# Gates of the dense tokens: from one-hot matrix products to an accumulating scatter by GpSimd

## The chip, the cores and the metric

One core of a Trainium2 chip runs the whole kernel. The metric is the device time of one execution in microseconds. Before the change it is 4364.05 us, the median of 3 runs (4363.18 to 4364.18).

## What is computed

One inference step of one layer for 576 tokens: 512 prompt tokens and 64 sample tokens, width 2048. Attention and a pooling branch come first; the change lies in the expert mixer behind them:

```python
s = einsum('nhcd,hckd->nhck', q, sub_keys)          # 8 heads, 2 halves, 128 keys
sv, si = top_k(s, 16)
cand = sv[:, :, 0, :, None] + sv[:, :, 1, None, :]  # 256 sums a head
top_s, top_p = top_k(cand, 16)
experts = take_along_axis(cidx, top_p)              # a * 128 + b, of 16384 experts
gate = softmax(top_s)
act = gelu(einsum('nd,nhkd->nhk', h, u[experts]))
out = einsum('nhk,nhkd->nd', gate * act, v[experts])
```

So each token has 8 x 16 = 128 chosen experts with a gate each. Two heads may choose the same expert; then their gates add up.

## The kernel before

The expert part treats the tokens in three ways. For the first 384 (**dense tokens**, TV) it computes the activation of all 16384 experts, multiplies it by a gate that is zero where an expert was not chosen, and multiplies that by all values. For tokens 384 to 447 it computes all activations too but picks single cells of them later. For the last 128 (N_SU) it gathers the 128 chosen rows of u and of v one row per token at a time.

**Expert stage.** 128 expert tiles (N_U), one for each second key b, each of 128 experts. For a tile SP loads 1 MB of u (line 577), VectorE turns it (`turn`, line 1643), ScalarE rounds it to the high part (line 1138), VectorE subtracts for the low part (`u_low`, line 1648), and TensorE runs 48 matmuls (`expert_tile`, line 2309) of 448 columns. ScalarE applies gelu and SP stores the result to gelu_dram (line 582). Everything is double buffered: u_high of tile n+1 waits for the matmuls of tile n-1. The parts stand in each engine's program in an order written out by hand.

In tiles 0 to 34, seven for each of the five blocks of 128 tokens, VectorE also does the selection (lines 1655 to 1716) in the order `SEL_ORDER = (3, 4, 0, 1, 2)`, a piece behind each half tile. The result for a block is `sel`: first key a, second key b and gate, token by chosen slot. TensorE turns each block (`turn_selected`, line 2325) and ScalarE copies it to iaT, ibT and gT.

From tile 36 on two things run beside the tiles:

- **Dots**: GpSimd gathers a row of u for each of 128 tokens (`gather_u`, line 791, a ring of 3 buffers; each gather waits for the dot that frees its buffer) and VectorE multiplies and sums it (`dot`, line 1778). `dots_of` spreads the 128 dots over 88 tiles (D_TILES).
- **Gate groups**: `groups_of` spreads 96 groups of 4 dense tokens over 83 tiles. VectorE writes, for each token, a one-hot matrix of a and a matrix of b weighted with the gate (lines 1766 and 1770). TensorE multiplies the two in the middle of an expert tile (`gate_matrix`, line 2344), which gives the token's 128x128 gates with equal experts summed. ScalarE copies the group out (`take_gates`, line 1170), and SP stores 48 pieces of 512 KB to gmat_dram (line 596).

**Value stage.** For each expert tile SP loads the gelu values and the gates of the dense tokens (lines 620 to 622), VectorE multiplies them (line 1810), and TensorE runs three matmuls of 384 columns for each of 16 output blocks (line 2387). GpSimd's gathers of rows and cells (lines 806 to 820) run beside it.

Ahead of the expert stage stand the branch products (16 weight tiles, G_BR), the output product (16, G_OUT) and the query product (16, G_PQ), whose weights SP loads in one sequence (`load_tile`).

Of the kernel before, what the change touches and what calls it, by code (L numbers as in the profile page):

```python
# [18 lines left out]
F = mybir.dt.float32  # L19
# [36 lines left out]
NTOK_G = 4  # L56
# [4 lines left out]
N_G = TV // NTOK_G  # L61
GB = 64
# [22 lines left out]
N_HALF = TV * 2 // GB  # L85
G_PER_HALF = GB // 2 // NTOK_G
G_TILES, D_TILES = 83, 88
# [7 lines left out]
def groups_of(n):  # L95
    n -= DOT_TILE
    return range(N_G * n // G_TILES, N_G * (n + 1) // G_TILES) if 0 <= n < G_TILES else ()


PIECES = {1 + [n for n in range(N_U) if g in groups_of(n)][0] + 1 + i: (m, i)  # L100
          for m in range(N_HALF) for g in [G_PER_HALF * (m + 1) - 1] for i in range(4)}


NQ, QR = 4, 32
H_EARLY = PK * GB // T
# [14 lines left out]
def hybrid_step(nc, x_prompt, x_sample, cache_k, cache_v, state_pool, page_table, norm1_g, w_in, b_gate,  # L120
# [4 lines left out]
    with ctx:  # L125
# [143 lines left out]
        ssum = r("ssum", [P, 2, PH])  # L269
        r = Region(x2, END)  # L270
        one_i = [r(f"one_i{s}", [P, NTOK_G, PK]) for s in range(2)]
        gate_j = [r(f"gate_j{s}", [P, NTOK_G, PK]) for s in range(2)]
        u_rows = [r(f"u_rows{i}", [P, D]) for i in range(U_RING)]
        assert r.at - BASE <= END - 4096
        gmat = [Region(A_MAIN + s * PK * GB * 2, A_RING)(f"gmat{s}", [P, PK, GB // 2]) for s in range(2)]
        turned = [Region(A_MAIN + PK * GB * 4, A_RING)("turned0", [P, KD // 2, P]), Region(END - 4096, END)("turned1", [P, KD // 2, P])]

# [9 lines left out]
        g_back = [None, r("g_back1", [P, N_HALF, 2, GB // 2])]  # L287
# [8 lines left out]
        g_back[0] = r("g_back0", [P, N_HALF, 2, GB // 2])  # L296
# [37 lines left out]
        gmat_dram = nc.dram_tensor("gmat_dram", [P, N_PAIR, N_HALF, 2, GB // 2], F).ap()  # L334
# [3 lines left out]
        u_tiles = peer_u.rearrange("l (e c j) d -> (l c) e j d", c=QR, j=PK)  # L338
        gelu_cells = gelu_dram.rearrange("j i t -> (j i t)").unsqueeze(1)
# [50 lines left out]
        oh_v, gm_mm, gm_ev = (sem(n) for n in ("oh_v", "gm_mm", "gm_ev"))  # L390
        gm_out = [sem(f"gm_out{s}") for s in range(2)]
# [140 lines left out]
        def _(sp):  # L532
# [58 lines left out]
            def store_gates(n):  # L591
                if n in PIECES:
                    m, piece = PIECES[n]
                    j, at = slice(piece * PK // 4, (piece + 1) * PK // 4), slice(piece * PK // 8, (piece + 1) * PK // 8)
                    sp.wait_ge(gm_ev, G_PER_HALF * (m + 1))
                    sp.dma_start(gmat_dram[:, at, m].rearrange("i j x t -> i j (x t)"),
                                 gmat[m % 2][:, j, :].rearrange("i (j x) t -> i j (x t)", x=2)).then_inc(gm_out[m % 2], 16)

            for n in range(N_U - 4):
                if n:  # L600
                    store_gelu(n - 1)
                sp.wait_ge(u_turn, 2 * (n + 3))
                load_u(n + 4, n % 2)
                store_gates(n)
            for n in range(N_U - 4, N_U - 2):
                store_gelu(n - 1)
                store_gates(n)
# [7 lines left out]
            def load_weights(k):  # L615
# [5 lines left out]
                sp.dma_start(g_back[k % 2][:, :, :, :], gmat_dram[:, k]).then_inc(ag_in[0], 16)  # L621
                sp.dma_start(a_back[1][:, :], gelu_dram[2 * k + 1][:, 0:TV]).then_inc(ag_in[1], 16)

            for s in range(2):
                sp.wait_ge(gm_out[s], 64 * (TV // GB))
# [49 lines left out]
        def _(pool):  # L675
# [91 lines left out]

            for s in range(2):
# [97 lines left out]
        def _(act):  # L866
# [284 lines left out]
            def take_selected(tb):  # L1151

                w = tokens(tb)
                act.wait_ge(sel_tmm, SEL_AT[tb] + 1)
# [9 lines left out]
            def take_gates(g):  # L1164

# [1310 lines left out]
```

## Time and profile before

| | us |
|---|---|
| runs, median of 3 | 4364.05 |
| span of the profiled execution | 4361.2 |
| TensorE busy | 4257.0 (98%) |
| VectorE busy | 2941.9 (67%) |
| ScalarE busy | 1218.7 (28%) |
| GpSimd busy | 742.2 (17%) |
| expert stage | about 1870 to 3190 |
| value stage | about 3190 to 4330 |

The span runs from the first to the last instruction of the profiled execution; that execution has no other time of its own, and its span is 2.9 us under the median of the runs. PE is TensorE's matmuls, PEld its weight loads, DVE VectorE, ACT ScalarE, POOL GpSimd, SP SyncE. The chain that ended last is followed back from the last instruction to whatever released it. Spans on GpSimd are rough. A number in brackets behind an instruction is the idle time before it and what ended that.

### The profile page before, as it was taken

The numbers are of one execution on the slowest core, as the hardware profiler recorded it, in microseconds if no ns is written. First come the engines' busy times: TensorE is split into PE (matmuls) and PEld (weight loads), VectorE is DVE, ScalarE is ACT, GpSimd is POOL, SyncE is SP. The second block draws the span as 40 slices with busy tenths as digits, with TensorE's granted clock in tenths as the row PEclk, the third lists the DMA queues.
The fourth block names the chain that finished last, engine by engine and source line by source line (L and its number), as shares of the span: only waits on it lengthen the run. The fifth ranks groups of instructions, "written<-read, shape, count | busy, mean of one in ns | idle before, by whom it ended". The sixth has DMA issues, their size and how long they took to land.

```text
span 4361.2 us, 67488 instructions
## 1 busy us (share of the span) xinstructions
PE 4257.0 (98%) x28439; PEld 4024.2 (92%) x28439; DVE 2941.9 (67%) x4423; ACT 1218.7 (28%) x1610; POOL 742.2 (17%) x745
## 2 busy tenths in 40 slices
PE   7999999999999989999999999999999999999998
PEld 7999888998899989989999999999989999999998
DVE  3232463322334356699989999999868888888887
ACT  3221353322212121123232222222222222222234
POOL 1001002332000000000011111111122443333320
PEclk9999999999999989999999999999999999999999
DMA  6433226676343544345589999999999999999993
GB/s 195 113 102 106 85 63 196 227 244 204 110 133 116 149 104 85 78 118 131 129 243 292 292 282 297 280 292 289 278 329 356 359 338 361 364 355 356 356 344 131
DMA packets 599373, 968.32 MB, mean 222 GB/s; under 512 B 143889, under 2 KB 406033, under 8 KB 565016
## 3 DMA queue, kind: packets, MB, share of 16 engines
q1 hardware_dynamic: 508560, 519.33, 41.9%
q0 software_dynamic: 84992, 434.18, 27.0%
q10 hardware_dynamic: 5520, 10.49, 0.8%
q8 instruction: 225, 3.69, 0.3%
q14 instruction: 76, 0.62, 0.0%
HBM read 873.63 MB, written 85.75 MB: 220 GB/s over the span
## 4 chain that ended last, share of the span: by engine, by line
PE 94%; DVE 3%; ACT 1%; issue 1%; DMA 1%; SPq 0%; ACTq 0%; DVEq 0%
PE pair L1968 29%; PE pair L2309 28%; PE pair L2387 24%; PE quad L1968 2%; PE pair L2344 2%; PE pair L1932 1%; PE quad L2369 1%; PE quad L1932 1%; PE quad L2139 1%; ACT w_hi L890 1%; PE pair L2004 1%; PE quad L2182 1%; PE quad L2279 0%; PE quad L2054 0%; SPq L534 0%
## 5 line engine op out<-in xcount | busy, mean ns | idle before, releaser
L2309 PE MATMUL pair<-act_hi,w_hi 128*128 128x448 f32 x2048 | 757.0, 370 | 4.4 <-DVE w_lo L1648 4.4
L2309 PE MATMUL pair<-act_lo,w_hi 128*128 128x448 f32 x2048 | 748.9, 366 | 0.0
L2309 PE MATMUL pair<-act_hi,w_lo 128*128 128x448 f32 x2048 | 748.6, 366 | 0.0
L1968 PE MATMUL pair<-act_hi,w_hi 128*128 128x288 f32 x3264 | 719.0, 302 | 29.2 <-DVE act_lo L1353 12.2
L1293 DVE TENSOR_TENSOR w_lo<-w_raw,w_hi 128x2048 fp32r<-128x2048 f32 x103 | 236.2, 2293 | 746.7 <-ACT w_hi L890 746.7
L1968 PE MATMUL pair<-act_hi,w_lo 128*128 128x288 f32 x3264 | 702.6, 297 | 0.0
L1968 PE MATMUL pair<-act_lo,w_hi 128*128 128x288 f32 x3264 | 701.3, 297 | 0.0
L2387 PE MATMUL pair<-wx_hi,v_hi 128*128 128x384 f32 x2016 | 678.8, 337 | 5.5 <-DVE wx_lo L1817 3.3
L2387 PE MATMUL pair<-wx_hi,v_lo 128*128 128x384 f32 x2016 | 674.7, 335 | 0.0
L2387 PE MATMUL pair<-wx_lo,v_hi 128*128 128x384 f32 x2016 | 674.6, 335 | 0.0
L1968 PEld LDWEIGHTS pair<-act_hi,w_hi 128*128 128x128 f32 x3264 | 526.3, 190 | 67.6 <-issue 61.4
L1968 PEld LDWEIGHTS pair<-act_lo,w_hi 128*128 128x128 f32 x3264 | 528.6, 190 | 0.0
L1968 PEld LDWEIGHTS pair<-act_hi,w_lo 128*128 128x128 f32 x3264 | 528.6, 190 | 0.0
L890 ACT CAST w_hi<-w_raw 128x2048 fp32r<-128x2048 f32 x112 | 213.6, 1907 | 829.8 <-PE pair L1968 727.9
L1194 ACT CAST v_hi<-v_raw 128x1024 fp32r<-128x1024 f32 x252 | 252.8, 1048 | 661.4 <-PE pair L2387 646.7
L2309 PEld LDWEIGHTS pair<-act_hi,w_hi 128*128 128x128 f32 x2048 | 385.4, 188 | 35.4 <-issue 4.0
L2309 PEld LDWEIGHTS pair<-act_hi,w_lo 128*128 128x128 f32 x2048 | 385.1, 188 | 31.0
L2309 PEld LDWEIGHTS pair<-act_lo,w_hi 128*128 128x128 f32 x2048 | 385.4, 188 | 29.5
L2387 PEld LDWEIGHTS pair<-wx_hi,v_hi 128*128 128x128 f32 x2016 | 379.3, 188 | 33.8 <-issue 30.3
L1832 DVE TENSOR_TENSOR main<-pair,main 128x384 f32<-128x384 f32 x528 | 292.2, 555 | 159.9 <-PE pair L2387 157.2
L2387 PEld LDWEIGHTS pair<-wx_lo,v_hi 128*128 128x128 f32 x2016 | 379.4, 188 | 0.0
L2387 PEld LDWEIGHTS pair<-wx_hi,v_lo 128*128 128x128 f32 x2016 | 379.3, 188 | 0.0
(339 smaller groups left out, 5467.3 us busy)
## 6 DMA issues: line engine op xcount, KB each, us to landing
w_raw<-in_peer_u_dram SPq DMA_DIRECT2D x512, 256.0 KB
v_raw<-in_peer_v_dram SPq DMA_DIRECT2D x256, 512.0 KB, 7.9
w_raw<-in_w_in_dram SPq DMA_DIRECT2D x64, 1024.0 KB
gelu_dram<-tmp SPq DMA_DIRECT2D x128, 224.0 KB, 7.5
gmat_dram<-gmat SPq DMA_DIRECT2D x48, 512.0 KB, 12.8
a_back<-gelu_dram SPq DMA_DIRECT2D x128, 192.0 KB, 6.6
g_back<-gmat_dram SPq DMA_DIRECT2D x64, 384.0 KB, 7.3
w_raw<-in_w_out_dram SPq DMA_DIRECT2D x16, 1024.0 KB
```

The lines of the kernel that those rows point to most:

```text
L890: a.copy(w_hi[g % 2][:, :, :], w_raw[g % 2][:, :, :]).then_inc(hi_done, 1)
L1194: a.copy(value_parts(n)[0][:, c], v_raw[i % V_RAWS][:, :]).then_inc(v_hid, 1)
L1293: v.tensor_sub(w_lo[g % 2][:, :, :], w_raw[g % 2][:, :, :], w_hi[g % 2][:, :, :].bitcast(F)).then_inc(lo_done, 1)
L1832: v.tensor_add(main[:, d, 0:TV], bank(d), main[:, d, 0:TV]).then_inc(acc_done, 1)
L1932: return nc.tensor.transpose(out, in_, ident[0:n, 0:n])
L1968: op = m_(pair[out][:, hf, 0:TH], w[:, k, :], x[:, k, hf * TH:(hf + 1) * TH], start=(starts and k == ks[0] and i == 0), stop=(ends and k = ...
L2004: op = m_(pair[t][:, hf, 0:TH], w[:, k, :], x[:, k, hf * TH:(hf + 1) * TH], start=(k == 0 and i == 0), stop=(k == KD - 1 and i == 2))
L2139: op = m_(pair[2][quadrant(j), s_, g * P:(g + 1) * P], qd[:, bp % 2, bb, s_ * COLS + j, :], kT_page[:, s_ * COLS + j, :], start=(bb == 0 a ...
L2182: op = m_(pair[3][j * QR:j * QR + DT, 1, s_ * P:(s_ + 1) * P], s_aT[:, bb, g, h * DT:(h + 1) * DT], v_page[m % V_RING][:, h * VD:(h + 1) * ...
L2309: op = m_(pair[0][:, n % 2, 0:TU], w[n % 2][:, k, :], x[:, k, 0:TU], start=(k == 0 and i == 0), stop=(k == KD - 1 and i == 2))
L2344: op = m_(pair[1][:, g % 2, n * PK:(n + 1) * PK], one_i[g % 2][:, n, :], gate_j[g % 2][:, n, :], start=True, stop=True)
L2387: op = m_(bank(d), w[:, c], x[:, :], start=(start and t == terms[0]), stop=(stop and t == terms[-1]))
```

## The change

GpSimd puts the gates of the dense tokens into gmat_dram itself. The table now has one cell for each expert and dense token, `[a, b, token]`. SP writes zeros to all of it, 48 stores of 512 KB from a zeroed buffer, two behind each of 24 weight loads of the branch and output products. After the selection of a dense block VectorE works out the cell numbers and copies the gates (`gate_cells`). Then one indirect transfer for each head and slot adds 128 gates, one per token, into their cells: 3 x 128 = 384 transfers. Since two heads can choose the same cell, a head's first transfer waits for all of the head before it in its block. Six heads of block 0 go out before the first row gather; the others stand three by three ahead of the row gathers. TensorE's groups, VectorE's one-hots, ScalarE's copies, SP's stores of gates, and four of the five turns of `sel` are gone.

```diff
-NTOK_G = 4
+N_DENSE = TV // P
+D_TILES = 88
+SLOT_N = PH * TOPK
+N_ZERO, Z0 = 48, G_BR + 4
+ZW = PK * TV // N_ZERO
+EARLY_HEADS = 6
+HEADS = ([(0, h) for h in range(PH)][EARLY_HEADS:EARLY_HEADS + 1] + [(1, 0), (2, 0)] + [(0, PH - 1)]
+         + [(b, h) for h in range(1, PH) for b in (1, 2)])
+PUTS = [(b, h, k) for b, h in HEADS for k in range(TOPK)]
+PUTS_PER_ROW = 3
...
-        gmat_dram = nc.dram_tensor("gmat_dram", [P, N_PAIR, N_HALF, 2, GB // 2], F).ap()
+        gmat_dram = nc.dram_tensor("gmat_dram", [P, PK, TV], F).ap()
+        gmat_cells = gmat_dram.rearrange("i j t -> (i j t)").unsqueeze(1)
...
             for g in range(2, G_U):
                 load_tile(g)
+                if g == Z0:
+                    sp.wait_ge(zeros_set, 1)
+                if Z0 <= g < Z0 + N_ZERO // 2:
+                    for z in (2 * (g - Z0), 2 * (g - Z0) + 1):
+                        sp.dma_start(gmat_dram.rearrange("i j t -> i (j t)")[:, z * ZW:(z + 1) * ZW], zeros[:, :]).then_inc(gates_zeroed, 16)
...
+            pool.wait_ge(sq_used["sub"], H)
+            g.memset(zeros[:, :], 0.0).then_inc(zeros_set, 1)
...
+            def put_gate(b, h, k):
+                if k == 0 and h:
+                    pool.wait_ge(gates_put[b], 16 * TOPK * h)
+                n = h * TOPK + k
+                pool.indirect_dma_start(out=gmat_cells, out_offset=bass.IndirectOffsetOnAxis(ap=g_idx[:, b, n:n + 1], axis=0),
+                                        in_=g_val[:, b, n:n + 1], in_offset=None, compute_op=ALU.add).then_inc(gates_put[b], 16)
+            pool.wait_ge(gates_zeroed, 16 * N_ZERO)
+            pool.wait_ge(gates_ready, 1)
+            for h in range(EARLY_HEADS):
+                for k in range(TOPK):
+                    put_gate(0, h, k)
             pool.wait_ge(top_done, N_PQ + 2)
-            pool.wait_ge(sel_tev, 3 * TB)
+            pool.wait_ge(gates_ready, N_DENSE)
             for i in range(U_RING):
                 gather_u(i)
             for i in range(U_RING, N_SU):
+                for b, h, k in PUTS[PUTS_PER_ROW * (i - U_RING):PUTS_PER_ROW * (i - U_RING + 1)]:
+                    put_gate(b, h, k)
                 pool.wait_ge(dot_done, DOT + i - U_RING + 1)
                 gather_u(i)
...
+            def gate_cells(tb):
+                link(v.scalar_tensor_tensor(tpf[:, 0, :], sel[:, 0, :], float(P), sel[:, 1, :], ALU.mult, ALU.add),
+                     v.tensor_scalar_add(g_col[:, tb:tb + 1], col_f[:, 0:1], float(tb * P)))
+                link(v.tensor_scalar(g_idx[:, tb, :], tpf[:, 0, :], float(TV), g_col[:, tb:tb + 1], ALU.mult, ALU.add))
+                dve.wait_ge(sel_done, SEL_AT[tb] + 1)
+                v.tensor_copy(g_val[:, tb, :], sel[:, 2, :]).then_inc(gates_ready, 1)
...
                     if k % 8 == 0:
                         pe.wait_ge(u_lo, n * 2 + 1 + k // 8)
-                    if k == KD // 2:
-                        for g in groups_of(n - 1):
-                            gate_matrix(g)
```

The functions one_hots, gate_matrix, take_gates and store_gates are removed with their calls, and the value stage reads its gates in the new layout, again 3072 contiguous bytes a partition for two tiles.

## Rows read from the trace of the kernel before

**Rows 1.** The page: span, TensorE, DMA in 40 slices, and the chain by engine.

```profile
span 4361.2 us, 67488 instructions
PE 4257.0 (98%) x28439; PEld 4024.2 (92%) x28439; DVE 2941.9 (67%) x4423; ACT 1218.7 (28%) x1610; POOL 742.2 (17%) x745
...
DMA  6433226676343544345589999999999999999993
...
PE 94%; DVE 3%; ACT 1%; issue 1%; DMA 1%; SPq 0%; ACTq 0%; DVEq 0%
```

**Rows 2.** The chain in order of time, 2000 to 2300 us: start, us, what.

```profile
2013.39 68.30 PE pair L2309 x336
...
2208.83 0.33 PE pair L1932 x3
2209.15 14.60 PE pair L2309 x72
2223.75 0.89 PE pair L2344 x8
2224.64 9.72 PE pair L2309 x48
2234.36 0.89 PE pair L2344 x8
```

**Rows 3.** ScalarE's copies of the gate groups: ns min/median/max, first and last start.

```profile
L1170 ACT COPY gmat<-pair x96: 586/587/590, 2224.7 to 3107.1; 128x512 f32<-128x512 f32 x96
```

**Rows 4.** Stages (selection, gate groups, values): busy us by engine, clock, DMA share, GB/s.

```profile
1900.00:2200.00 300.00, 300.00 (x1483) 276.80 (x1482) 289.64 (x451) 89.81 (x117) 0.00 (x0) 1.00 0.54 132
2240.00:3100.00 860.00, 860.00 (x4576) 803.17 (x4575) 792.37 (x1025) 248.24 (x332) 139.26 (x117) 1.00 0.99 289
3300.00:4200.00 900.00, 900.00 (x5312) 850.78 (x5311) 778.95 (x919) 247.92 (x304) 334.12 (x305) 1.00 0.95 356
```

**Rows 5.** VectorE by form, 2215 to 3107 us: busy us, mean ns, idle before.

```profile
L1778 DVE CUSTOM_DVE_ANT_0 u_rows<-quad,u_rows 128x2048 f32<-128x2048 f32 x121 | 273.8, 2286 | 1.9 <-DMA u_rows<-in_peer_u_dram,e_slot 1.9
L1643 DVE STREAM_TRANSPOSE turned<-w_raw 128x1024 f32<-128x1024 f32 x167 | 208.0, 1245 | 9.7 <-DMA w_raw<-in_peer_u_dram 4.0
L1648 DVE TENSOR_TENSOR w_lo<-turned,w_hi 128x1024 fp32r<-128x1024 f32 x166 | 199.8, 1204 | 63.0 <-ACT w_hi L1138 62.5
```

**Rows 6.** GpSimd in order of time, four stretches.

```profile
1172.31 0.54 POOL L774 DMA_DIRECT2D back<-gate_dram  x1 [7.61 <-DVE act_lo L1568]
...
2210.68 0.99 POOL L791 DMA_INDIRECT u_rows<-in_peer_u_dram,e_slot  x1 [400.40 <-ACT gT L1156]
2211.98 0.99 POOL L791 DMA_INDIRECT u_rows<-in_peer_u_dram,e_slot  x1 [0.30 <-issue]
...
2403.32 1.68 POOL L791 DMA_INDIRECT u_rows<-in_peer_u_dram,e_slot  x1 [1.26 <-DVE s_act L1778]
...
3215.06 0.95 POOL L806 DMA_INDIRECT e_act<-gelu_dram,e_cell  x1 [0.30 <-issue]
3216.32 0.96 POOL L806 DMA_INDIRECT e_act<-gelu_dram,e_cell  x1 [0.30 <-issue]
...
3402.67 2.90 POOL L806 DMA_INDIRECT e_act<-gelu_dram,e_cell  x1 [0.30 <-issue]
```

**Rows 7.** VectorE and ScalarE in order of time, four places.

```profile
2064.39 0.29 DVE L1704 TENSOR_TENSOR sel<-sel,ssum 128x128 f32<-128x128 f32 x1
...
2218.93 0.55 ACT L1144 ACTIVATE tmp<-pair 128x448 f32<-128x448 f32 x1 [7.13 <-PE pair L2309]
...
2402.97 1.22 DVE L1648 TENSOR_TENSOR w_lo<-turned,w_hi 128x1024 fp32r<-128x1024 f32 x1
...
3402.41 2.34 DVE L1826 SCALAR_TENSOR_TENSOR s_sum<-s_rows,s_act,s_sum 128x2048 f32<-128x2048 f32 x1
```

**Rows 8.** From issue to landing, us min/median/max: e_act (floats), then u_rows (rows).

```profile
DMA to landing us min/median/max: 4.0/6.7/9.7
...
DMA to landing us min/median/max: 6.3/8.6/13.8
```

**Rows 9.** VectorE by form, 1870 to 2210 us.

```profile
L1682 DVE TENSOR_TENSOR oh<-tpf,iota_f 128x2048 f32<-128x2048 f32 x8 | 18.2, 2271 | 0.1
L1659 DVE TENSOR_TENSOR cand<-sv 128x2048 f32<-128x2048 f32 x3 | 6.8, 2280 | 0.0
```

**Rows 10.** The page's DMA issues: KB each, us to landing.

```profile
gmat_dram<-gmat SPq DMA_DIRECT2D x48, 512.0 KB, 12.8
```

More of the change, by code:

```diff
@@ L92, in dots_of @@
     return range(N_SU * n // D_TILES, N_SU * (n + 1) // D_TILES) if 0 <= n < D_TILES else ()
[L95 to L101, printed above, removed]
 NQ, QR = 4, 32
-H_EARLY = PK * GB // T
+H_EARLY = 14
 COLS = 4
@@ L389, in hybrid_step @@
         hT_saved, hT_back = [sem(f"hT_saved{s}") for s in range(2)], sem("hT_back")
-        oh_v, gm_mm, gm_ev = (sem(n) for n in ("oh_v", "gm_mm", "gm_ev"))
-        gm_out = [sem(f"gm_out{s}") for s in range(2)]
+        zeros_set, gates_zeroed, gates_ready = sem("zeros_set"), sem("gates_zeroed"), sem("gates_ready")
+        gates_put = [sem(f"gates_put{b}") for b in range(N_DENSE)]
         u_turn, u_hi, u_lo, a_done, a_gelu = (sem(n) for n in ("u_turn", "u_hi", "u_lo", "a_done", "a_gelu"))
@@ L589, in _ @@
                 load_u(n, n % 2)
[L591 to L597, printed above, removed]
             for n in range(N_U - 4):
@@ L620, in load_weights @@
                 sp.dma_start(a_back[0][:, :], gelu_dram[2 * k][:, 0:TV]).then_inc(ag_in[0], 16)
-                sp.dma_start(g_back[k % 2][:, :, :, :], gmat_dram[:, k]).then_inc(ag_in[0], 16)
+                sp.dma_start(g_back[k % 2][:, :, :], gmat_dram[:, 2 * k:2 * k + 2, :]).then_inc(ag_in[0], 16)
                 sp.dma_start(a_back[1][:, :], gelu_dram[2 * k + 1][:, 0:TV]).then_inc(ag_in[1], 16)
-            for s in range(2):
-                sp.wait_ge(gm_out[s], 64 * (TV // GB))
+            for b in range(N_DENSE):
+                sp.wait_ge(gates_put[b], 16 * SLOT_N)
             for s in range(2):
@@ L1757, in _ @@
                     expert_slots(tb)
-            def one_hots(g):
-                if g == 0:
-                    dve.wait_ge(sel_tev, 3 * TB)
-                if g >= 2:
-                    dve.wait_ge(gm_mm, g - 1)
-                at, full = slice(g * NTOK_G, (g + 1) * NTOK_G), [P, NTOK_G, PK]
-                v.tensor_tensor(one_i[g % 2][:, :, :], iota_f[:, :].unsqueeze(1).broadcast_to(full),
-                                iaT[:, at].unsqueeze(2).broadcast_to(full), ALU.is_equal)
-                for n in range(NTOK_G):
-                    t = g * NTOK_G + n
-                    op = v.tensor_scalar(gate_j[g % 2][:, n, :], iota_f[:, :], ibT[:, t:t + 1], gT[:, t:t + 1], ALU.is_equal, ALU.mult)
-                op.then_inc(oh_v, 1)
+                else:
+                    gate_cells(tb)
             def dot(i):
@@ L2334, in turn_selected @@
                 op.then_inc(sel_tmm, 1)
-            def gate_matrix(g):
-                pe.wait_ge(oh_v, g + 1)
-                if g >= 2:
-                    pe.wait_ge(gm_ev, g - 1)
-                else:
-                    pe.wait_ge(sel_tev, 3 * TB)
-                for n in range(NTOK_G):
-                    op = m_(pair[1][:, g % 2, n * PK:(n + 1) * PK], one_i[g % 2][:, n, :],
-                            gate_j[g % 2][:, n, :], start=True, stop=True)
-                op.then_inc(gm_mm, 1)
             pe.wait_ge(sc_ev, 2 * N_PQ)
@@ L2352, in _ @@
                 q, i = divmod(n, SEL_TILES)
-                if 1 <= q <= TB and i == (1 if q < TB else 0):
-                    turn_selected(SEL_ORDER[q - 1])
+                if q == 1 and i == 1:
+                    turn_selected(SEL_ORDER[0])
                 if n < 4:
```

56 lines of the change are left out of this document (19 added, 37 removed).

## The prediction

> **What bounds the kernel now.** I read the page first, then the chain of waits in order of time, then the stages, then the single instructions of the engines that the change loads. The page says that TensorE is busy for 98% of a span of 4361.2 us and makes up 94% of the chain that ended last [rows 1]. So time taken from TensorE is time won, until another engine is late. The profiled execution's span is 4361.2 us; the median of the runs is 4364.05 us, 2.9 us above it. No other time of that execution is shown, so I make the sum as a difference and lay it on the median.
>
> The chain in order of time shows the stage that the change touches [rows 2]. Until 2223.75 us it is expert tiles alone, each 48 matmuls of line 2309: 68.30 us for 336 matmuls is 9.76 us a tile, and one tile alone takes 9.73 us. From then on a gate group of 0.89 us (line 2344) stands between two half tiles. All of it is TensorE; nothing in the stage waits for data. ScalarE's row counts 96 such groups [rows 3].
>
> **What is removed.** A group costs the step between two group starts less one tile: 2234.36 - 2223.75 - 9.73 = 0.88 us, on the path each time. 96 x 0.885 = 85.0 us. Four of the five turns of selected gates go too; each is a piece of 0.33 us on the chain [rows 2], 1.3 us. Together **-86.3 us**. ScalarE's 96 copies, VectorE's one-hot rows and SP's 48 stores of 512 KB [rows 3, 10] go as well. They are worth nothing by themselves, since TensorE does not wait for them, but they make room.
>
> **Is TensorE still last at 9.73 us a tile?** VectorE keeps per tile two subtractions (1.20), two transposes (1.25) and 128/88 = 1.45 dots (2.29 plus about 0.09 to read the sum) [rows 5]: 2.4 + 2.5 + 3.45 = 8.35 us. It has 1.4 us to spare, so I cost it at nothing; if dots come late, this cover is gone, because VectorE works in order and the next tile's low parts stand behind the dot. The three new gate_cells (four operations on 128x128 or less, about 1 us each, my estimate from the 0.29 us of line 1704 [rows 7]) fall into the selection stage, in which VectorE is busy 289.6 of 300 us [rows 4], about 2.4 us idle in each block of seven tiles. I take 1 us in all.
>
> **The zeroed table.** 48 stores of 512 KB go out with 24 weight tiles of the branch and output products, 25.2 MB, which is what the gate stores moved. At the rate of the value stage, 356 GB/s at 0.95 of the engines' time, thus 375 GB/s when full [rows 4], they need 67 us of all engines, spread over some 24 tiles of 13 us, in slices where the engines are 0.3 to 0.7 busy [rows 1]. Two more stores per tile on SP's queue stand behind that tile's load and before the next, which waits for a buffer anyway. The memset on GpSimd stands before the loads of the gates; the wait for those loads' permission is 7.6 us long [rows 6]. Bounds 0 and 10 us (one late load); I take 0, as the nearest slices are far from full.
>
> **The early puts.** No row shows an accumulating scatter. The nearest is the gather of 128 single floats (line 806): GpSimd 0.95 us and 1.26 us from start to start; a gather of whole rows costs the same, 1.30 us [rows 6]. So size does not matter there and 128 indices do. I take 1.24 us for a put, from the bound below; the bound above, twice the busy part, is 2.2 us. One thing lengthens it: at 2403.32 a gather took 1.68 us, at 3402.67 2.90 us [rows 6]. Beside them stand VectorE's operations with two SBUF operands, 2402.97 to 2404.19 and 3402.41 to 3404.75 [rows 7]: GpSimd ends 0.8 us after each. So a put that starts beneath such an operation waits for its end.
>
> 96 puts (six heads of block 0) start when block 0's gates are ready, 2064.39 + 0.29 + about 1 us = 2066 us [rows 7]. 96 x 1.24 = 119 us. In the 150 us that follow VectorE runs some 30 subtractions of 1.2 us and 10 operations of 2.27 us like lines 1682 and 1659 [rows 7, 9]; each catches one start, for about 0.5 and 1.0 us more: 25 us. Five times a head waits until the one before has landed. A gather of floats lands in 4.0 to 9.7 us after issue [rows 8] under full engines; here they are 0.54 busy [rows 4], so I take 5, that is 3.8 us beyond the 1.24: 19 us. Sum 163 us: the first row gather goes out at 2229 us instead of 2210.68 [rows 6]. It lands 8.6 us later [rows 8], at 2238. Without cost the first dot could have waited until 2225: TensorE ends tile 36 at 2218.9 [rows 7] and tile 37 at 2228.6, and dot (2.3) and subtraction (1.2) must fit before. The rest, 13 us, stalls VectorE and then TensorE. I take **+12 us**; bounds 0 (landing in 2 us) and 35 (landing in 9.7).
>
> The Trainium skill, page "DMA: Bandwidth & Descriptors", section "Anatomy of one DMA", gives a fixed cost of some 2 us for a small transfer. The rows above, 4.0 us at the least, do not agree. By that page the first row gather would go out at 2214, this term would be 0 and the time 4284 us.
>
> **The steady puts.** 288 puts lie in the first 96 rows, 66 tiles. Per tile GpSimd then issues 4.36 puts and 1.45 row gathers, 5.8 x 1.24 = 7.2 us, and two subtractions hold it 0.5 us each: 8.2 us of 9.73. The row ring is three deep: a gather may go out 19.5 - 8.6 = 11 us after the dot that frees its buffer, and at most one row's three puts (3.7 us) stand before it. The head waits lie over five rows behind the puts they ask for, so are over. **0 us.**
>
> The DMA engines are 0.99 busy in that stage at 289 GB/s [rows 4]. A tile there lasts 9.73 + 0.885 x 96/83 = 10.75 us, 10.6 us of engine work. The expert weights and gelu stores are 0.54 x 9.73 = 5.25 us, the row gathers 1.45 x 1.05 MB at 375 GB/s 4.07 us; 1.3 us remain for the gate store, 303 KB in pieces of 256 B, 74 pieces an engine, 17 ns each. After the change 9.3 of 9.73 us are taken, and 558 put elements, 35 an engine, come on top. At 12 ns each they just fit; at 17 ns they need 0.6 us, 0.2 us a tile too much, 13 us in 66 tiles. Bounds 0 and the rival below; I take **+5 us**.
>
> Sum: -86 + 1 + 12 + 5 = -68: **4296 us**.
>
> **Rivals.**
> (1) The puts cost what I say but the early ones are further behind (landing near 9.7 us, or VectorE holds more): 4296 to 4345 us. For it: five serial waits. Against: the engines are half idle.
> (2) **The pace of GpSimd decides; slower.** Accumulating may need more work for each index than gathering. With 1.5 us busy a put the cadence is 1.8: early 173 + 25 + 16 us, a stall of about 55; steady 4.36 x 1.8 + 1.8 + 1.0 = 10.65 us a tile, 0.92 x 66 = 61 us. 4364 - 86 + 1 + 116 = 4395 us. With a doubled put (1.9) it is about 4550 us. It decides from 1.3 us busy and turns the sign at about 1.4. For it: no row shows such a put, and the margin is half its price. Against: the two kinds of gather, with 4 B and 8 KB an index, cost the same.
> (3) **The DMA engines decide; slower.** An element that is read, added and written takes longer than a 256-byte piece. At 50 ns: 35 x 0.05 = 1.75, 11.05 us a tile, +1.3 x 66 = 87 us, 4378 us. At 100 ns: 12.8 us, +203 us, 4494 us. The sign turns at about 44 ns. For it: 0.99 busy before. Against: 17 ns for the nearest piece.
> The same page, section "Specifications", says that transfers under 512 B are read, modified and written; that speaks for this rival. The 256-byte pieces are under that size too and take 17 ns here.
> (4) Nothing moves, because VectorE at 8.35 us or a late weight load takes the place of the groups: 4355 to 4370 us. The 68.30 us for seven tiles, with VectorE busier than it will be, speak against it.
>
> **How the numbers follow.** Forecast (4278 to 4300) 0.42; (1) 0.15; (2) 0.21; (3) 0.17; (4) 0.05. A change of 0.2%, 9 us, is about what a measurement of this kernel can tell from none. Faster: the forecast, (1), and 0.02 of the milder ends of (2) and (3): 0.59. Within 0.2%: 0.05. Slower: 0.36. The range starts at 4274, the removed work with nothing given back, and must take in (1), (4) and more than half of (2) and (3): up to 4430, which leaves out about 0.15. Of the likeliest case alone the range is 4276 to 4302 us.
>
> **What would show it.** Right: tiles of 9.73 us in the chain without line 2344, no wait of VectorE on u_rows after the first, GpSimd's puts at a median of 0.95 us. Early term: one wait of the first dot of about 15 to 20 us near 2219 us. Rival (2): puts with a median over 1.3 us and tile steps over 10 us for 66 tiles, then 9.73. Rival (3): the same steps with puts at 0.95 us, DMA share at 1, and waits on w_raw or u_rows. A branch or output stage that is longer than before would show the zero stores in the way.

## The result, and the profile after

| | before | after |
|---|---|---|
| runs, median of 4, us | 4363.61 | 4401.5 |
| runs, lowest to highest, us | 4355.79 to 4364.18 | 4397.02 to 4418.26 |
| profiled execution, us | not shown | 4418.26 |
| its span, us | 4361.2 | 4416.1 |

The changed kernel is slower: 1.0097 times the time of before, 95% interval 1.0083 to 1.011, 38 us. The profiled execution is the slowest of the four, 17 us above their median. Its span is 54.9 us above that of before, and the traces are compared on that.

The page of the changed kernel: span, engines, DMA share in 40 slices, chain by engine, two groups of part 5 and one DMA issue:

```profile
span 4416.1 us, 65628 instructions
PE 4207.6 (95%) x27659; PEld 3954.8 (90%) x27659; DVE 2790.7 (63%) x3955; ACT 1166.0 (26%) x1502; POOL 1396.0 (32%) x1130
...
DMA  6433226776365633356659999999989999999993
...
PE 73%; POOL 14%; DVE 4%; issue 4%; DMA 3%; ACT 1%; SPq 0%; ACTq 0%; DVEq 0%; POOLq 0%
...
L2299 PE MATMUL pair<-act_hi,w_hi 128*128 128x448 f32 x2048 | 763.4, 373 | 109.9 <-DVE w_lo L1649 106.5
L796 POOL DMA_INDIRECT gmat_dram<-g_val,g_idx x384 | 647.2, 1685 | 396.1 <-DVE g_val L1724 256.3
...
gelu_dram<-tmp SPq DMA_DIRECT2D x128, 224.0 KB, 13.6
```

Against [rows 1]: TensorE is 49 us less busy and the span 55 us longer. GpSimd, 17% busy before and not in the chain's first shares, is 32% busy and makes up 14% of the chain. TensorE now waits for w_lo for 106.5 us. The stores of gelu land 13.6 us after issue (median), where the page of before has 7.5.

The puts (line 796) and the row gathers (line 787) of the changed kernel, all stages: duration ns min/median/max, first and last start, then what the engine waited for before them and from issue to landing:

```profile
L796 POOL DMA_INDIRECT gmat_dram<-g_val,g_idx x384: 1540/1559/3575, 2066.4 to 2999.8; - x192
...
  DMA gmat_dram<-g_val,g_idx: 17.4, 5
...
DMA to landing us min/median/max: 2.9/8.6/20.3
```

```profile
L787 POOL DMA_INDIRECT u_rows<-in_peer_u_dram,e_slot x128: 936/997/2046, 2283.7 to 3190.5; - x128
...
  DMA u_rows<-in_peer_u_dram,e_slot: 230.6, 58
...
DMA to landing us min/median/max: 5.5/13.8/22.5
```

A put takes 1559 ns at the median and a gather still 997. The first row gather starts at 2283.7 us instead of 2210.68 [rows 6], and dots wait for rows 58 times, 230.6 us in all. GpSimd of the changed kernel in order of time (start, duration, what, idle before and what ended it):

```profile
2066.44 1.86 POOL L796 DMA_INDIRECT gmat_dram<-g_val,g_idx  x1 [256.32 <-DVE g_val L1724]
...
2074.61 1.55 POOL L796 DMA_INDIRECT gmat_dram<-g_val,g_idx  x1 [0.30 <-issue]
2076.47 1.54 POOL L796 DMA_INDIRECT gmat_dram<-g_val,g_idx  x1 [0.30 <-issue]
...
2142.86 1.55 POOL L796 DMA_INDIRECT gmat_dram<-g_val,g_idx  x1 [6.32 <-DMA gmat_dram<-g_val,g_idx]
...
2283.72 1.00 POOL L787 DMA_INDIRECT u_rows<-in_peer_u_dram,e_slot  x1 [0.30 <-issue]
...
2298.77 2.41 POOL L796 DMA_INDIRECT gmat_dram<-g_val,g_idx  x1 [0.30 <-issue]
2301.49 1.53 POOL L787 DMA_INDIRECT u_rows<-in_peer_u_dram,e_slot  x1 [0.30 <-issue]
2303.32 1.57 POOL L796 DMA_INDIRECT gmat_dram<-g_val,g_idx  x1 [0.30 <-issue]
...
2307.06 1.55 POOL L796 DMA_INDIRECT gmat_dram<-g_val,g_idx  x1 [0.30 <-issue]
2308.92 0.99 POOL L787 DMA_INDIRECT u_rows<-in_peer_u_dram,e_slot  x1 [0.30 <-issue]
```

From start to start a put costs 1.85 us (1.86 in this pair). Until the first row gather there is one put behind the other. After it, rows come 7.43 us apart (2301.49 to 2308.92) with three puts between two of them, and GpSimd is idle there only for the 0.30 us that every issue has. From 2295 to 2936 us it waits for dots 7 times, 6.6 us in all. The consequence on VectorE, in the same trace:

```profile
2289.33 2.29 DVE L1774 CUSTOM_DVE_ANT_0 u_rows<-quad,u_rows 128x2048 f32<-128x2048 f32 x1 [75.16 <-DMA u_rows<-in_peer_u_dram,e_slot]
...
2291.55 1.22 DVE L1649 TENSOR_TENSOR w_lo<-turned,w_hi 128x1024 fp32r<-128x1024 f32 x1
```

The first dot waits 75.16 us. The low part of the next tile stands behind it in VectorE's order, so TensorE has no weights. The stage by stretches, changed kernel, then the same work before (window, length, busy us of PE, PEld, DVE, ACT, POOL, granted clock, DMA share, GB/s):

```profile
2208.80:2295.00 86.20, 20.47 (x97) 18.65 (x96) 10.46 (x9) 5.28 (x7) 65.31 (x44) 0.62 0.39 66
2295.00:2936.00 641.00, 601.28 (x2829) 545.16 (x2828) 472.26 (x408) 147.28 (x177) 529.83 (x344) 0.97 1.07 257
2936.00:3245.10 309.10, 309.10 (x1490) 280.89 (x1490) 239.87 (x217) 77.88 (x96) 96.95 (x66) 0.99 0.97 279
```

```profile
2208.80:3189.80 981.00, 981.00 (x5190) 915.60 (x5189) 875.75 (x1111) 282.31 (x378) 151.32 (x128) 1.00 0.99 287
```

97 + 2829 + 1490 = 4416 matmuls are 92 tiles. Before, the same tiles with the matmuls of 96 gate groups took 981.0 us; now they take 1036.3 us, 55.3 us more, which is the whole difference of the spans. It divides so:
- **-86.3 us**, the groups and turns removed;
- **+65.7 us**, TensorE idle around the first dot (86.20 - 20.47);
- **+67.6 us** in the second stretch, 641.0 us for 58.9 tiles, 10.88 us a tile, against 58.9 x 9.73. Of it 39.7 us are idle, and 27.9 us are matmuls that step by 212.5 ns (601.28/2829) instead of 202.7;
- **+7.1 us** in the third, where TensorE is never idle and each step takes 207.4 ns.

The sum is +54.1; another 0.8 us are the longer steps of the first stretch (20.47 us for 97 matmuls). Part of the longer steps is the granted clock after each wait. Windows of the changed kernel at the end of the long one:

```profile
2279.00:2291.00 12.00, 0.00 (x0) 0.00 (x0) 1.67 (x1) 0.00 (x0) 9.87 (x8) 0.50 0.57 160
2291.00:2310.00 19.00, 17.09 (x72) 15.75 (x73) 18.83 (x18) 4.52 (x5) 15.87 (x11) 0.81 0.98 279
2310.00:2330.00 20.00, 20.00 (x100) 18.56 (x100) 15.04 (x14) 4.85 (x6) 16.73 (x11) 1.00 1.11 267
```

While TensorE stood idle, the granted clock was at the lower level, 0.50 (1.2 GHz); over the 19 us after the restart its mean is 0.81, then it is 1.00. The third stretch has a longer step at a mean clock of 0.99; that is taken up below.

Elsewhere nothing moved. In the branch and output products, where the table is zeroed, 230 us before and after (columns as above, before first):

```profile
1370.00:1600.00 230.00, 210.81 (x1551) 209.27 (x1550) 86.82 (x85) 43.61 (x35) 9.12 (x17) 0.96 0.51 139
```

```profile
1370.00:1600.00 230.00, 210.73 (x1550) 209.20 (x1548) 86.94 (x85) 43.62 (x35) 9.13 (x17) 0.95 0.59 183
```

TensorE does the same work while the DMA share goes from 0.51 to 0.59, and the expert stage starts at 1863.85 us before and 1863.69 us after. The value stage from 3300 to 4200 us has 900.00 us of TensorE and 356 GB/s in both.

### The profile page after: what moved, and what is told of

Read it like the earlier page. It is cut to its first block, busy times and chain, and to the rows that moved or that the text cites. A ratio compares the mean times of both kernels' runs of the same rounds, so it can differ in the third digit from the quotient of the medians.

```text
span 4416.1 us, 65628 instructions
## 1 busy us (share of the span) xinstructions
PE 4207.6 (95%) x27659; PEld 3954.8 (90%) x27659; DVE 2790.7 (63%) x3955; ACT 1166.0 (26%) x1502; POOL 1396.0 (32%) x1130
## 3 DMA queue, kind: packets, MB, share of 16 engines
q0 software_dynamic: 140288, 434.41, 30.5%
## 4 chain that ended last, share of the span: by engine, by line
PE 73%; POOL 14%; DVE 4%; issue 4%; DMA 3%; ACT 1%; SPq 0%; ACTq 0%; DVEq 0%; POOLq 0%
PE pair L1961 29%; PE pair L2362 24%; POOL gmat_dram L796 12%; PE pair L2299 10%; PE quad L1961 2%; DMA u_rows<-in_peer_u_dram,e_slot 2%; POOL u_rows L787 2%; PE pair L1925 1%; PE quad L2344 1%; PE quad L1925 1%; PE quad L2132 1%; ACT w_hi L901 1%; PE pair L1997 1%; PE quad L2175 1%; DMA gmat_dram<-g_val,g_idx 1%
## 5 line engine op out<-in xcount | busy, mean ns | idle before, releaser
L2299 PE MATMUL pair<-act_hi,w_hi 128*128 128x448 f32 x2048 | 763.4, 373 | 109.9 <-DVE w_lo L1649 106.5
L796 POOL DMA_INDIRECT gmat_dram<-g_val,g_idx x384 | 647.2, 1685 | 396.1 <-DVE g_val L1724 256.3
L2299 PE MATMUL pair<-act_lo,w_hi 128*128 128x448 f32 x2048 | 760.7, 371 | 0.0
L2299 PE MATMUL pair<-act_hi,w_lo 128*128 128x448 f32 x2048 | 760.4, 371 | 0.0
L1774 DVE CUSTOM_DVE_ANT_0 u_rows<-quad,u_rows 128x2048 f32<-128x2048 f32 x128 | 290.5, 2274 | 230.7 <-DMA u_rows<-in_peer_u_dram,e_slot 230.6
## 6 DMA issues: line engine op xcount, KB each, us to landing
gelu_dram<-tmp SPq DMA_DIRECT2D x128, 224.0 KB, 13.6
```

Of the source, the lines that this page charges most:

```text
L796: pool.indirect_dma_start(out=gmat_cells, out_offset=bass.IndirectOffsetOnAxis(ap=g_idx[:, b, n:n + 1], axis=0), in_=g_val[:, b, n:n + 1], ...
L1774: v.tensor_tensor_reduce(out=u_rows[i % U_RING][:, :], in0=quad[:, :, :].rearrange("p a c -> p (a c)"), in1=u_rows[i % U_RING][:, :], scal ...
L2299: op = m_(pair[0][:, n % 2, 0:TU], w[n % 2][:, k, :], x[:, k, 0:TU], start=(k == 0 and i == 0), stop=(k == KD - 1 and i == 2))
```

## The experiments

Two theories stood against each other. **The pace of GpSimd:** a put costs 1.85 us of the issuing engine, early puts and row gathers queue behind one another. **The DMA engines:** they are near full, and added elements make rows, weights or gelu stores late. Each kernel was timed beside the kernel before, whose median lay between 4363 and 4377 us from one set of runs to the next; so ratios are compared, each to the kernel before in its own set. The diffs are against the changed kernel, unless said otherwise. Those that leave work out are named there.

**Plain puts.** The transfer writes instead of adding; where two heads choose the same cell, the last gate stays instead of the sum.

```diff
-                                        in_=g_val[:, b, n:n + 1], in_offset=None, compute_op=ALU.add).then_inc(gates_put[b], 16)
+                                        in_=g_val[:, b, n:n + 1], in_offset=None).then_inc(gates_put[b], 16)
```

> Leaves out the addition: each put is a plain scatter, so a gate is lost where two heads chose the same expert. Theory P (the pace of GpSimd: an accumulating put keeps it busy 1.55 us where a gather takes 0.95): if the addition is what costs, a put falls to about 0.95 us, the first dot waits under 20 us instead of 75, and the time is 4290 to 4310 us. If scattering costs and adding does not, the put stays at 1.55 and the time at 4400. Theory D (the DMA engines are full with the put's small elements): the steps of the tiles stay well over 9.73 us for 66 tiles even with cheap puts, 4330 to 4350 us.

4333.87 us, ratio 0.9903 (0.9887 to 0.992). The puts:

```profile
L796 POOL DMA_INDIRECT gmat_dram<-g_val,g_idx x384: 963/972/3003, 2071.7 to 2914.4; - x192
```

972 ns, as a gather [rows 6]. So scattering costs GpSimd no more than gathering, and the addition alone costs 0.59 us. The first row gather starts at 2229.6 us, and no dot waits for a row. By the two ratios the kernel is 1.9% faster than the changed one, some 85 us.

It does not reach the forecast. TensorE is busy 623.28 of 640 us from 2260 to 2900, and 68.34 of the 80 us from 2040 to 2120. But from 1900 to 3190 us it never waits for w_lo: its idle time among the expert tiles, 28.7 us in 40 pieces of at most 2.4 us, has no releaser that the trace shows. So the trace shows neither theory at work there, and the cause is open; the profiled execution is the slowest of the four, 14 us above the median. This edit does not separate the theories either, since it relieves both. Over the whole page the queue of GpSimd moves 84992 packets before, 140288 with adding puts and 97280 with plain ones: 144 packets for an adding put of 128 gates, 32 for a plain one.

**Puts spread.** Four heads early and the other 320 puts over all 125 rows, 2.56 a row; the order of the later heads changes with it. Nothing is left out.

```diff
-EARLY_HEADS = 6
-HEADS = ([(0, h) for h in range(PH)][EARLY_HEADS:EARLY_HEADS + 1] + [(1, 0), (2, 0)] + [(0, PH - 1)]
-         + [(b, h) for h in range(1, PH) for b in (1, 2)])
+EARLY_HEADS = 4
+HEADS = [(b, h) for h in range(PH) for b in ((0, 1, 2) if h < PH - EARLY_HEADS else (1, 2))]
+HEADS = [(b, h + EARLY_HEADS if b == 0 else h) for b, h in HEADS]
...
-                for b, h, k in PUTS[PUTS_PER_ROW * (i - U_RING):PUTS_PER_ROW * (i - U_RING + 1)]:
+                for b, h, k in PUTS[len(PUTS) * (i - U_RING) // (N_SU - U_RING):len(PUTS) * (i - U_RING + 1) // (N_SU - U_RING)]:
```

> Same puts, four early heads instead of six, and the other 320 puts spread evenly over all 125 row gathers (2.56 a row instead of 3). Theory P: 64 early puts end near 2215 us, so the first dot waits under 15 us; per tile 3.72 x 1.86 + 1.45 x 1.3 + 1.0 = 9.8 us on GpSimd, just the tile; 4290 to 4310 us. Theory D: 41 put transfers and the row gathers still overfill the engines, tiles of 10 us and more over all 88 tiles: 4325 to 4350 us.

4356.27 us, 0.9955 (0.994 to 0.9971). The first dot waits 11.8 us instead of 75, and GpSimd now waits for dots, so it has time left. The longest waits of this kernel from 2300 to 2900 us (who waited for what: total, times, longest; others between these are left out):

```profile
ACT tmp L1155 <- DMA gelu_dram<-tmp: 236.7, 33, 9.4
POOL u_rows L787 <- DVE s_act L1774: 83.1, 38, 6.4
DVE turned L1644 <- DMA w_raw<-in_peer_u_dram: 72.9, 31, 6.0
DVE u_rows L1774 <- DMA u_rows<-in_peer_u_dram,e_slot: 69.1, 30, 6.1
```

and the window from 2260 to 2900 us:

```profile
2260.00:2900.00 640.00, 606.32 (x2890) 552.32 (x2889) 476.63 (x412) 151.90 (x180) 471.07 (x313) 0.98 1.08 264
```

TensorE is still idle 34 us; the profiled execution is 10 us above the median of the ten. Weights, rows and above all gelu stores are late, at a DMA share of 1.08. That is the mark of the second theory; the kernel with rows of half the length, below, tests it.

**Each term alone.** The first kernel leaves the 288 later puts out, the second the 96 early ones (those gates stay zero); waits for puts that are gone are adapted too, which the diffs leave out.

```diff
-                for b, h, k in PUTS[PUTS_PER_ROW * (i - U_RING):PUTS_PER_ROW * (i - U_RING + 1)]:
+                for b, h, k in PUTS[:0][PUTS_PER_ROW * (i - U_RING):PUTS_PER_ROW * (i - U_RING + 1)]:
```

> Leaves out the 288 puts among the row gathers, keeps the 96 early ones. The early stall alone: TensorE waits 66 us, so 4363 - 86 + 66 = 4343 us (both theories). If the 9.9 us tiles seen after the stall come from the puts, they are back at 9.73 here; if they come from the stall, they stay and the time is 4358.

```diff
-            for h in range(EARLY_HEADS):
-                for k in range(TOPK):
-                    put_gate(0, h, k)
```

> Leaves out the 96 early puts, keeps the 288 at three a row. No wait before the first dot. Theory P: 4363 - 86 + 66 tiles x (4.36 x 1.86 + 1.9 + 1.0 - 9.73 = 1.3 us) less what the ring gives = 4340 to 4360 us, and TensorE's idle time stands under waits of VectorE on u_rows. Theory D: the same time, but with landings of w_raw late too; if the engines are not the limit, landings of rows stay near 8.6 us.

Early puts alone: 4368.37 us, 0.9977 (0.9964 to 0.999); the whole wait of the first dot is there, and from 2300 to 2900 us TensorE has no idle time. Later puts alone: 4341.99 us, 0.9933 (0.9915 to 0.9952); no long wait, and TensorE idle for 31 of 640 us:

```profile
2260.00:2900.00 640.00, 609.13 (x2926) 554.76 (x2925) 485.34 (x419) 152.10 (x183) 533.29 (x351) 0.98 1.02 266
```

So either term is there without the other: against the 86 us removed, the early puts give back 81 us on the median and the later ones 54 us. Together that is 135 us, where the changed kernel gives back 124.

**Puts of 64 tokens.** The second half of each block's gates is left out; the number of puts stays.

```diff
-                pool.indirect_dma_start(out=gmat_cells, out_offset=bass.IndirectOffsetOnAxis(ap=g_idx[:, b, n:n + 1], axis=0),
-                                        in_=g_val[:, b, n:n + 1], in_offset=None, compute_op=ALU.add).then_inc(gates_put[b], 16)
+                pool.indirect_dma_start(out=gmat_cells, out_offset=bass.IndirectOffsetOnAxis(ap=g_idx[0:NS, b, n:n + 1], axis=0),
+                                        in_=g_val[0:NS, b, n:n + 1], in_offset=None, compute_op=ALU.add).then_inc(gates_put[b], 16)
```

> The changed kernel with each put reduced to 64 tokens instead of 128 (the other half of the dense gates is left out); as many puts. If the time of a put on GpSimd goes with its indices, the busy time falls from 1.55 to about 1.2 us or less; if it is fixed, it stays. Theory P: early stall down from 66 to about 30 us or less when the put is 1.2. Theory D: half the elements leave the engines with about 9.5 of 9.73 us a tile, so the later idle time of TensorE (40 us between 2300 and 2940) mostly goes. Both together: ratio 0.985 to 0.995.

4366.48 us, 0.9986 (0.9977 to 0.9996), above the expected range. With half the elements a put takes 1431 ns instead of 1559. A line through these two points gives 2 ns an index and 1.3 us fixed, an estimate: the price is one of the number of puts. 384 puts that are 0.128 us cheaper make 49 us, and the two ratios differ by 48 us. That fits the pace of GpSimd, but the DMA elements are halved too, so this run does not separate the theories.

**Rows of half the length.** On the spread kernel, a row gather brings 4 KB instead of 8 KB an index (half of each dot's sum is left out), so the DMA engines are relieved and GpSimd issues exactly the same. Three memsets of 0.91 us on VectorE clear the other halves once, ahead of the first dot; the diff leaves them out.

```diff
-                pool.indirect_dma_start(out=u_rows[i % U_RING][:, :], out_offset=None, in_=u_rows_dram,
+                pool.indirect_dma_start(out=u_rows[i % U_RING][:, 0:D // 2], out_offset=None, in_=u_half_dram,
```

> e2_spread with row gathers of half length (4 KB instead of 8 KB for each token; the dots see zeros in the other half, so part of the sums is left out). GpSimd issues as much as in e2_spread, the DMA engines carry 0.76 MB less a tile. Theory P (pace of GpSimd): TensorE's losses between 2300 and 3140 us stay as in e2_spread, ratio about 0.995. Theory D (the engines are full, so that gelu stores, weights and rows land late): the losses go, ratio 0.982 to 0.986.

4308.77 us, 0.9846 (0.983 to 0.9862).

```profile
2260.00:2900.00 640.00, 640.00 (x3159) 593.21 (x3158) 530.28 (x455) 159.63 (x197) 524.18 (x343) 1.00 0.93 212
```

In this window TensorE is never idle, where the spread kernel has 34 us of idle time; by the ratios the edit is worth 1.1%. So in the spread kernel the late transfers were what held TensorE. The profiled execution is the fastest of the five, 4284.34 us; the other four took 4308 to 4311, and their traces are not kept. The same edit on the changed kernel, three puts a row:

> The changed kernel (six early heads, three puts a row) with row gathers of half length, as in e6_short_rows, so the DMA engines have room; GpSimd issues exactly what it does in the changed kernel. In e6, with 2.56 puts a row, all idle time was gone. Theory P for this density: 4.36 x 1.87 + 1.45 x 1.3 + 1.0 = 11 us of GpSimd a tile, so VectorE still waits for rows (100 us or more between 2300 and 2900) and TensorE is idle for 20 to 40 us there; ratio 1.000 to 1.006. Theory D: idle time gone behind the first stall as in e6, ratio 0.996 to 1.000.

4397.87 us, 1.0074 (1.0057 to 1.0091), against 1.0097 without it.

```profile
2260.00:2900.00 640.00, 581.80 (x2761) 530.17 (x2762) 469.57 (x405) 143.31 (x173) 533.83 (x349) 0.95 0.85 186
```

```profile
DVE u_rows L1775 <- DMA u_rows<-in_peer_u_dram,e_slot: 133.4, 42, 5.9
```

The window takes in the end of the long wait, as does the same one of the changed kernel, with 571.59 us of TensorE. The DMA share is down to 0.85 and a row lands in 6.5 us at the median instead of 13.8, and yet dots wait for rows 42 times from 2300 to 2900 us, as in the changed kernel (133.0 us, 47 times). The intervals of the two ratios overlap. So at three puts a row the pace of GpSimd holds TensorE by itself. These two edits settle the question: GpSimd is the limit of the change as made, the DMA engines the next.

**Another order of the blocks.** The dense blocks are selected at places 0, 2 and 4 of the order instead of 2 to 4, so puts start at 1937 us; seven heads go early and 272 puts are spread, 2.2 a row. Nothing is left out.

```diff
-SEL_ORDER = (3, 4, 0, 1, 2)
+SEL_ORDER = (0, 3, 1, 4, 2)
...
+EARLY = [(0, 0), (0, 1), (0, 2), (0, 3), (1, 0), (0, 4), (1, 1)]
```

> Complete computation. Block 0 is selected first (order 0, 3, 1, 4, 2), so puts can start at about 1935 us: 7 heads go out before the first row gather, the other 272 puts are spread over 125 rows (2.2 a row). Theory P: 3.17 x 1.86 + 1.9 + 1.0 = 8.8 us a tile of GpSimd, under 9.73, no early stall: ratio 0.981 to 0.985, faster than before and than all others. Theory D: 3.17 puts a tile still put the engines at 1.0, late gelu stores go on: ratio 0.985 to 0.993.

4340.88 us, 0.9921 (0.9904 to 0.9938), in the range expected if the DMA engines are the limit. The gelu stores hold ScalarE longest (284.2 us, 36 times, from 2300 to 2900), so the next kernel adds a third gelu buffer to it, in space free at that time:

```diff
+            return gelu_third[:, :] if n % 3 == 2 else tmp[:, n % 3, 0:TU]
...
-                if n >= 2:
-                    act.wait_ge(a_out[n % 2], 16 * (n // 2))
+                if n >= 3:
+                    act.wait_ge(a_out[n % 3], A_BASE[n % 3] + 16 * (n // 3))
```

> e8_reorder with a third buffer for gelu's result, so ScalarE's next gelu no longer waits for the store of two tiles before but of three. Theory P: nothing changes, as e8. Theory D with the gelu stores as the place where late landings hurt: 0.981 to 0.984, and the waits of ScalarE's gelu on its stores are gone.

4327.71 us, 0.9906 (0.9876 to 0.9935), short of the expected 0.981 to 0.984 but the best complete version: about 1% under the kernel before and 1.9% under the changed one. Windows of both, from 2260 to 2900 us, without and with the third buffer:

```profile
2260.00:2900.00 640.00, 615.11 (x2950) 560.49 (x2949) 484.54 (x422) 153.89 (x183) 423.70 (x283) 0.98 1.06 268
```

```profile
2260.00:2900.00 640.00, 629.08 (x3059) 574.31 (x3058) 504.27 (x438) 157.19 (x190) 452.05 (x296) 1.00 1.08 278
```

The idle time falls from 24.9 to 10.9 us, the share stays above 1, and what is late now is loads of w_raw (96.6 us, 36 times; 121.2 us, 41 times, without the third buffer). The intervals of the two ratios overlap, so the gain in total time is likely but not shown.

**A wait in the kernel before.** Against the kernel before, GpSimd does 40 memsets ahead of its first row gather; nothing else changes.

```diff
+            for i in range(40):
+                g.memset(u_rows[0][:, :], 0.0).then_inc(held, 1)
+                pool.wait_ge(held, i + 1)
             for i in range(U_RING):
                 gather_u(i)
```

> The kernel before with one artificial stall: 40 memsets on GpSimd (about 2 us each) ahead of its first row gather, nothing else changed. Tests whether one stall of TensorE by itself leaves the tiles behind it at 9.9 us in place of 9.73. If so: the wait of the first dot (60 to 80 us) plus about 15 us, ratio 1.018 to 1.022, with expert tiles of 9.9 us to the end of the stage. If the slower tiles came from the puts: wait alone, ratio about 1.016.

4441.3 us, 1.0149 (1.0132 to 1.0166): a wait of 71 us of the first dot costs 64 us of time, so hardly more than TensorE's idle time of 65 us. Its chain in order of time has the step of before again at once:

```profile
2301.29 9.73 PE pair L2313 x48
2311.02 0.89 PE pair L2348 x8
```

**The longer step.** After its one wait, the kernel with early puts alone has no idle time to the end of the stage, and yet 9.94 us a tile. The next kernel is the same with one 128x128 transpose of the identity (into a PSUM buffer that is free by then) in every fourth tile from tile 40 on:

```diff
+                    if k == KD // 2 and n >= 40 and n % 4 == 0:
+                        tr(pair[1][:, 0, 0:P], ident[:, :])
```

> e3_early_only with one 128x128 transpose of the identity in the middle of every fourth expert tile from tile 40 on. In e3_early_only all 90 tiles behind the one stall took 9.9 us; in e10_stall_in_before, with gate products between the tiles, they went back to 9.73. If an instruction of another form between the matmuls ends the slower step, tiles go back to 9.73 at the first transpose and the ratio falls from 0.9977 to about 0.994 (22 transposes of 0.1 us are 2 us of it). If not, the ratio stays at 0.998.

4357.07 us, 0.9965 (0.9953 to 0.9976), against 0.9977 (0.9964 to 0.999); the intervals overlap. The chains in order of time, early puts alone, then with transposes, then the kernel with half-length rows, whose TensorE waited for w_lo once, 1.4 us:

```profile
2298.76 894.90 PE pair L2298 x4320
```

```profile
2297.12 27.07 PE pair L2300 x120
...
2324.30 38.90 PE pair L2300 x192
```

```profile
2229.74 875.77 PE pair L2303 x4320
```

4320 matmuls in 894.90 us are 207.2 ns each; 192 in 38.90 are 202.6, and so are the 4320 in 875.77 (202.7). This pair does not show that the transposes end the longer step: in the trace with transposes the starts of the matmuls are 202.7 ns apart from 2304.57 us on, 20 us ahead of the first transpose at 2324.20, so the longer step never set in behind the wait.

Other rows do show it. The kernel before has the longer step at the start of its expert stage, 240 matmuls in 49.78 us or 207.4 ns each, and the shorter one from the first `turn_selected` on (line 1932, three transposes):

```profile
1894.86 49.78 PE pair L2309 x240
1944.64 0.33 PE pair L1932 x3
1944.97 68.09 PE pair L2309 x336
```

The kernel with another order of the blocks has that turn seven tiles later, and there the longer step lasts seven tiles longer, 576 matmuls at 207.0 ns:

```profile
1903.27 119.22 PE pair L2298 x576
2022.49 0.33 PE pair L1924 x3
2022.82 252.93 PE pair L2298 x1248
```

The kernel before has no long wait of TensorE ahead of it: its waits from 1800 to 1870 us are 4.4 us in two. So a long wait is not needed for the longer step, and in these traces three transposes end it.

The best version with the same transposes:

> e9_reorder_ring3 with the same transposes. If they end the slower steps of 9.9 us: 5 to 12 us less than e9, ratio 0.987 to 0.990. If not: as e9 or 2 us more, ratio 0.990 to 0.992.

4329.17 us, 0.9913 (0.988 to 0.9946): no difference from it that can be measured. It has many short waits and its clock stays at 0.99 to 1.00 from 2260 to 2900 us.

## Why the prediction failed

The forecast was 4296 us and faster; measured is 4401.5, inside the range of 4274 to 4430 and on the other side of before.

- **What is removed, -86.3 us: right.** The tile step falls to 9.73 us wherever nothing is late: 875.77 us for 90 tiles with half-length rows.
- **VectorE at 8.35 us a tile, gate_cells +1 us: right.** From 1900 to 2200 us TensorE is busy for all 300 us, as before; with half-length rows and nothing late VectorE has 8.1 us a tile.
- **The zeroed table, 0 us: right**, by the windows from 1370 to 1600 us.
- **The early puts, +12 us: the step that failed, by the price of a put.** I took 1.24 us from start to start, from the gathers, with 2.2 as the other end; it is 1.85. 96 x 1.85 = 178 us instead of 119. The rest of the term held: from 2066.44 to 2283.72 are 217.3 us, so blocked starts and head waits took 39.7 us (17.4 of them the five head waits), and I had 25 + 19. The start was 2066, as said, and the first gather came at 2283.7 instead of 2229. The cost is 66 us. All of the 54 us too much is in 96 x 0.61 = 59.
- **The steady puts, 0 us: failed by the same price.** With 1.85 the step's own sum is 4.36 x 1.85 + 1.45 x 1.30 + 1.0 = 11.0 us of GpSimd a tile, and 10.88 us from tile to tile are measured. In the profiled execution the step costs 68 us of the second stretch, part of it the longer step and the clock. My cover was 1.5 us a tile, and a put 0.34 us dearer used it up; I had written that half the price was the margin and had given the price a chance of 0.21 to be off.
- **Blocked starts: right.** The put at 2298.77 took 2.41 us; beside it stands VectorE's subtraction with two SBUF operands, 2298.54 to 2299.76. The Trainium skill, page "SBUF — State Buffer", section "SBUF: two separate sides", says that such an operation and one of GpSimd that reads SBUF exclude each other for a whole instruction. This trace agrees: the put ends 1.42 us behind the subtraction, nearly the 1.56 us of a put. The prediction had read 0.8 us from two gathers.
- **The DMA engines, +5 us: too small, but hidden in the result.** That they decide the time of the change as made is not shown: relieving them alone gave 0.2%, within the intervals. Where the pace is relieved, late transfers cost 34 us of idle time in 640 (puts spread). Two sizes of the step were off. An element, priced at 12 to 17 ns, takes 26 ns: that is the mean of the packets of 4 bytes in GpSimd's queue of the changed kernel from 2300 to 2900 us. With it the step's own sum is 9.3 + 35 x 0.026 = 10.2 us a tile and 32 us in all, an estimate. And the 0.4 us of room a tile was no measure. The kernel with early puts alone and transposes has neither gate stores nor puts in that stretch, and its DMA share is 1.00 from 2300 to 2900 us, with TensorE busy for all 600.
- **Landing.** The puts' landing, which I took as 5 us for the early ones, is 2.9/8.6/20.3 us over all of them; the five waits for it cost 17.4 us, about the 19 of the sum. The Trainium skill, page "DMA: Bandwidth & Descriptors", section "Anatomy of one DMA", has 2 us for a small transfer; no put came under 2.9 us.

**Rival (2)** named the place, the mechanism and the price: at 1.5 us busy, 55 us early, 61 us steady, 4395 us; measured 1.56 us, 66 and 68 us in the profiled execution, 4401.5 us for the median. Its 55 does not follow from its own terms: 173 + 25 + 16 is 51 us more than the forecast's 163, which makes a stall of 64 us, and about 4404 us in all. Its marks, puts over 1.3 us and tiles over 10 us, then shorter tiles again, are in the trace, but the shorter ones take 9.96 us (309.10 us for 1490 matmuls) and not 9.73. **Rival (3)** is half true: its marks stand beside rival (2)'s in the changed kernel already, at a DMA share of 1.07 from 2300 to 2900 us (waits of 133.0 us on u_rows, 79.3 on gelu stores and 17.4 on w_raw), but they decide only once GpSimd has time, and its price of 44 ns an element or more was not met. Removing 86 us from TensorE uncovered two queues, one behind the other. With the addition's price gone (plain puts) the kernel stands at 0.9903. With the addition kept, the puts spread and the rows halved, it stands at 0.9846, which is 67 us, about the forecast's 68; that kernel leaves work out, so the agreement is no proof of the sum.

## What to carry to other kernels

- An operation of which the trace shows only a relative is priced with the relative as the lower end. When the issuing engine's cover is smaller than the distance between the ends, the dearer end is the forecast, or the operation is measured first: one kernel with a plain put instead of an adding one gave the price here.
- Work moved from a full engine to an idle one is a question of order as well as of share: GpSimd was only 32% busy over the span, but between 2066 and 3000 us it did nothing but issue, save for some 24 us of waits, and the row gathers stood in the same queue. Start such work earlier, spread it evenly between what is urgent, and then count the next resource.
- A DMA share near 1 does not by itself say whether anything is late. The stage of before has 0.99 and early puts with transposes 1.00, both with TensorE never idle; with added puts at 1.06 to 1.08 it is idle 11 to 34 us of 640. Look at the waits: the stores of gelu, with two buffers, were the longest wait, and a third buffer came with 14 us less idle time.

## What had not been expected of the hardware

- **Adding in a scatter costs the issuing engine, not just the transfer.** 0.59 us of GpSimd for each put, nearly the same for 64 and 128 indices (1.43 and 1.56 us).
- **Two steps of the same matmul at full clock.** Matmuls of 448 columns step by 202.7 ns in some stretches and by about 207.2 in others, for up to 890 us on end, both at a granted clock of 1.00. The kernel before has both: 207.4 ns until the first three transposes of selected gates, 202.7 after. Moving that turn by seven tiles moved the change of step with it. The 32 matmuls of `turn_h` ahead of each stretch did not end it. What starts the longer step is open. It follows the long wait in the kernel with early puts alone, and not in the one with transposes, though its first transpose comes 20 us later. The kernel with early puts alone was timed ten times: four times at 4353 to 4356 us and six at 4367 to 4373; with transposes all seven lie at 4352 to 4362. The kernel with half-length rows, without a long wait, has one at 4284 and four at 4308 to 4311. Such a step in some executions and not in others would explain both pairs, since it is worth 19 us, but only one execution of each shows its steps, so it isn't shown.
- **The clock's way back.** After the long wait TensorE restarts at the lower level of the clock (a mean of 0.81 over the first 19 us, above). After the one long wait of the kernel with transposes the first 120 matmuls took 27.07 us, where 120 at 202.7 ns take 24.3: 2.8 us. Many short waits add up: in the second stretch of the changed kernel 2829 matmuls at 207.2 ns would take 586.2 us and took 601.3, at a mean granted clock of 0.97, so by this count some 15 us went there beside 40 us of idle time.
